# Four recurrent heads in straight-line code, with the next head's projections between the steps of the current one

## What is computed

```
mq, mk = split(silu(centred_short_conv(concat(ml_q, ml_k), conv_w, conv_b)))     # 5 taps in time
h_fwd, h_bwd = mlstm_chunkwise(...), flip(mlstm_chunkwise(flip(...)))              # per head:
    C_new = decay * C + einsum('s,se,sd->ed', w, v_c, k_c)                         #   recurrence over chunks
    S = (q @ k.T) * exp(Dlog - m_t)
    h = (S @ v + inter * (C_prev @ q)) / max(|den|, exp(-m_t))
hm = (h_fwd + h_bwd) * sigmoid(ml_o)
hm = (hm - mean) * rsqrt(var + EPS) * ml_norm_w                                    # per head
ml_out = hm * silu(ml_z)
```

## Time and profile before

| | us |
|---|---|
| three runs | 3822.88, 3825.00, 3828.41 (median 3825.0) |
| the profiled execution | 3826.68, its span 3824.6 |
| `mlstm` in the span: first DMA issue to the next stage's first DMA issue | 193.43 to 1038.64 |
| first matmul of each head | 211.43, 416.98, 625.10, 833.48 |
| TensorE busy over the whole span | 3479.6 (91%) |

### The profile page before, as it was taken

The page is one execution under the profiler, slowest core; times in us unless marked ns, Lnnn a source line. Parts: engine busy times, 40 slices in busy tenths (PEclk is TensorE's granted clock), DMA queues, the critical chain, the costliest instruction groups (busy, mean ns, idle before and its releaser), DMA issues. The chain is left out here.

```text
span 3824.6 us, 43828 instructions
## 1 busy us (share of the span) xinstructions
PE 3479.6 (91%) x16583; PEld 1882.9 (49%) x16583; DVE 1142.0 (30%) x2614; ACT 1013.8 (27%) x2401; POOL 706.5 (18%) x602
## 2 busy tenths in 40 slices
PE   6479797979699999989899999999999999989899
PEld 3238484746545545444445454454545444544444
DVE  3322324142403213154423233242333223211132
ACT  3202112131313324133223342252334233301000
POOL 0010102020100000053331124114211511300143
PEclk9689898989899999999899999999999999999999
DMA  6021001000221010133215615353542445332221
GB/s 226 7 48 28 23 19 29 17 29 23 44 67 32 17 31 18 14 117 102 70 31 34 37 52 88 42 38 85 51 30 43 109 31 40 101 108 92 92 80 67
DMA packets 295199, 211.39 MB, mean 55 GB/s; under 512 B 133401, under 2 KB 261928, under 8 KB 290090
## 3 DMA queue, kind: packets, MB, share of 16 engines
q1 hardware_dynamic: 288726, 198.13, 26.5%
q10 hardware_dynamic: 6272, 10.49, 0.8%
HBM read 166.96 MB, written 41.62 MB: 55 GB/s over the span
## 5 line engine op out<-in xcount | busy, mean ns | idle before, releaser
L1906 PE MATMUL d<-hT,w_tiles 128*128 128x512 f32 x1280 | 584.0, 600 | 9.8 <-DMA qk_w<-in_k_norm_w 9.8
L989 PE MATMUL n<-hT,wo 128*128 128x512 f32 x1024 | 453.4, 601 | 21.5 <-issue 11.6
L1906 PE MATMUL d<-w_room,w_tiles 128*128 128x512 f32 x960 | 433.8, 594 | 0.0
L1906 PEld LDWEIGHTS d<-hT,w_tiles 128*128 128x128 f32 x1280 | 244.5, 192 | 313.2 <-issue 301.5
L563 PE MATMUL m<-hT,w 128*128 128x512 f32 x768 | 341.4, 608 | 34.9 <-PEq L473 18.9
L989 PEld LDWEIGHTS n<-hT,wo 128*128 128x128 f32 x1024 | 194.6, 193 | 259.9 <-issue 248.3
L1906 PEld LDWEIGHTS d<-w_room,w_tiles 128*128 128x128 f32 x960 | 180.6, 190 | 220.6 <-issue 218.8
L563 PEld LDWEIGHTS m<-hT,w 128*128 128x128 f32 x768 | 149.5, 195 | 224.8 <-issue 224.8
L568 PEld LDWEIGHTS m<-w,hT 128*128 128x128 f32 x2048 | 229.3, 192 | 1.9 <-issue 1.9
L568 PE MATMUL m<-w,hT 128*128 128x128 f32 x2048 | 229.3, 275 | 0.0
L2980 PE MATMUL f<-hT,w_tiles 128*128 128x512 f32 x512 | 221.3, 593 | 5.2 <-ACT mid_out L2830 4.0
(11 more groups left out here) (351 smaller groups left out, 4535.9 us busy)
## 6 DMA issues: line engine op xcount, KB each, us to landing
w_tiles<-in_w_in SPq DMA_DIRECT2D x80, 256.0 KB, 2.9
trig<-in_trig SPq DMA_DIRECT2D x16, 1024.0 KB, 5.0
ada<-in_w_ada SPq DMA_DIRECT2D x6, 2048.0 KB, 19.7
mix_f<-alpha SPq DMA_DIRECT2D x64, 192.0 KB, 6.4
w<-in_w_in SPq DMA_DIRECT2D x20, 512.0 KB, 3.6
xg<-in_x ACTq DMA_DIRECT2D x4, 2048.0 KB, 23.4
rb<-r_rows SPq DMA_DIRECT2D x16, 512.0 KB, 5.4
wo<-in_w_in SPq DMA_DIRECT2D x16, 512.0 KB, 3.7
```

What stands on the lines that cost most here:

```text
L989: last = nc.tensor.matmul(bank[b][:], w[:, s, k], hT[:, k, tb * TB:(tb + 1) * TB], start=(k == 0), stop=(k == KC - 1))
L1906: last = nc.tensor.matmul(bank[self.bank_of(n, j, i)][:], w[:, k], x[k], start=(k == 0), stop=(k == h - 1))
```

## The change

- The loop over heads becomes straight-line code inside one block. Semaphores count on over all four heads, and the barrier, the clearing and the POOL copies between heads go.
- K, Q and Z of the next head are projected between the current head's steps: two units after each of the 15 recurrence products and after each of the 16 chunks (62 units), then 26 units up to the end of tile 10, then two after each of the four blocks of output transposes (8 units). V and O stay behind the tail, as a solid piece. The first head's K, Q and Z stay in one piece, and the last head has nothing to project beside it.
- ACT's evictions of those tiles go between its weighings and chunks: K and Q tiles 0 to 6 there, tile 7 and the first Z tile before the Sqrt of the tail, the other three Z tiles behind it.
- DVE's convolution of the next K goes between the normalisation and the multiplication into `mix`; the one of the next Q between the evictions of V.
- The output transposes use banks 2 and 3 instead of 0 and 1. O's weights go into a part of `mix` that is not yet written.
- The constants come as 18 rows in 4 DMAs, and TensorE turns them onto the partitions. Weights of the first head are loaded one by one by SP, K first, and each is waited for only by its user.

```diff
-            def _(act):
-                for s in range(O_):
-                    act.dma_start(w[:, s], w_v[:, :, (col[s] + 1) * HALF - P:(col[s] + 1) * HALF]).then_inc(consts, 16)
-                for n, row in enumerate(rows):
-                    sp.dma_start(small[:, :, n], row.rearrange("(h p) -> p h", p=P), **slow).then_inc(consts, 16)
+                load(0, K_)
+                sp.dma_start(ident[:], t["ident"]).then_inc(consts, 16)
...
+                for n, rows in ((0, b_rows), (5, w_rows), (15, c_rows), (17, t["ml_norm_w"])):
+                    sp.dma_start(small_rows[n:n + rows.shape[0]], rows).then_inc(consts, 16)
+                for s in range(Q_, NW):
+                    load(0, s)
...
-        with nc.Fori(0, ML_HEADS) as back:
...
-            clear(nc, sems, w_in[0])
+                pe.wait_ge(consts, 5 * 16)
+                for h in range(ML_HEADS):
+                    last = nc.tensor.transpose(bank[2][:, 18 * h:18 * h + 18], small_rows[:, h * P:(h + 1) * P], ident[0:18, 0:18])
+                last.then_inc(small_turned, 1)
+                project(0, 0, NA * KC)
+                for x in range(ML_HEADS):
+                    for n in range(NA, NB):
+                        project_turned(x, n)
+                    pe.wait_ge(k_ready, x + 1)
+                    turn(x, 0)
+                    at = 0
+                    for i in range(NS):
+                        if i + 1 < NS:
+                            turn(x, i + 1)
+                        product(x, i)
+                        project(x + 1, at, at + 2)
+                        at += 2
...
+                    for c in range(NT):
+                        if c + 1 < NT:
+                            scores(x, c + 1)
+                        cross(x, c)
+                        within(x, c)
+                        project(x + 1, at, at + 2)
+                        at += 2
+                    project(x + 1, at, 11 * KC)
                     for b in range(NTB):
+                        turn_out(x, b)
+                        project(x + 1, 11 * KC + 2 * b, 11 * KC + 2 * b + 2)
...
+            def _(act):
+                    for i in range(NS):
+                        weigh(x, i)
+                        if i > 3 and i % 4 == 0:
+                            evict(x + 1, i // 4 - 1)
+                    exps(x, 0)
+                    for c in range(NT):
+                        if c + 1 < NT:
+                            exps(x, c + 1)
+                        scale_cross(x, c)
+                        if c % 4 == 2:
+                            evict(x + 1, 3 + c // 4)
+                    evict(x + 1, 7)
+                    evict(x + 1, 8)
+                    act.wait_ge(stat, 2 * NT * (x + 1))
+                    nc.scalar.activation(rs[:, 0], mv[:, :, 1], ACT.Sqrt, bias=epst[:, 0:1]).then_inc(rooted, 1)
+                    for n in range(9, NA):
+                        evict(x + 1, n)
```

More of the change, by code:

```diff
@@ L401, in mlstm @@
     L = P + 1
+    NS = NT - 1
+    LAST = ML_HEADS - 1
+    heads = list(range(ML_HEADS))[::-1]
     with ExitStack() as ctx:
@@ L483, in _, with load @@
-                sp.dma_start(causal[:], t["causal"]).then_inc(consts, 16)
-                sp.wait_ge(consts, 24 * 16)
-            @block.scalar
-            def _(act):
-                for s in range(O_):
-                    act.dma_start(w[:, s], w_v[:, :, (col[s] + 1) * HALF - P:(col[s] + 1) * HALF]).then_inc(consts, 16)
+                def load(x, s):
+                    if x > LAST:
+                        return
+                    if s == O_ and x == LAST:
+                        sp.wait_ge(proj, NB * x + 4)
+                    elif x > 0:
+                        sp.wait_ge(proj, NB * (x - 1) + 4 * s + 4)
+                    c0 = col[s] * HALF + heads[x] * P
+                    sp.dma_start(weights(x, s), w_v[:, :, c0:c0 + P]).then_inc(w_in[s], 16)
@@ new lines, in _ @@
+                for s in range(Q_, NW):
+                    load(0, s)
+                sp.dma_start(causal[:], t["causal"]).then_inc(causal_in, 16)
+                fetch_bias(0)
+                fetch(0, 0)
+                fetch(0, 1)
+                for x in range(ML_HEADS):
+                    if x == 0:
+                        for s in range(V_):
+                            load(1, s)
+                    if x < LAST:
+                        load(x + 1, V_)
+                        load(x + 1, O_)
+                    fetch_bias(x + 1)
+                    if x < LAST:
+                        load(x + 2, K_)
+                    fetch(x, 2)
+                    fetch(x, 3)
+                    fetch(x + 1, 0)
+                    fetch(x + 1, 1)
+                    if x < LAST:
+                        load(x + 2, Q_)
+                        load(x + 2, Z_)
@@ L542, in _ @@
+                pool.wait_ge(causal_in, 16)
+                for x in range(ML_HEADS):
                     for b in range(NTB):
[L543 to L546, removed]
+                        mask(x, b)
@@ L581, in _ @@
                     for i in range(NS):
                         if i + 1 < NS:
[L583 to L600, removed]
-                    need(pe, carried, 2 * NS)
+                            turn(x, i + 1)
@@ L607, in _ @@
-                        nc.tensor.matmul(bank[4 + c % 2][:, 0:2 * L], qT[:, c * P:(c + 1) * P], state[:, c].rearrange("p d l -> p (d l)"), start=True, stop=True).then_inc(crossed, 1)
-                        need(pe, scored, c + 1)
-                        need(pe, summed, max(c - 1, 0))
-                        for dr in range(2):
-                            last = nc.tensor.matmul(bank[6 + c % 2][:, dr * L:(dr + 1) * L], sd[:, c % 2, dr], v1[:, c], start=True, stop=True)
-                        last.then_inc(inside, 1)
@@ L613, in _ @@
-                    for b in range(NTB):
-                        need(pe, normed, 4 * b + 4)
-                        if b < 2:
-                            need(pe, out_dve, 8)
-                        else:
-                            need(pe, h_out, b - 1)
-                        for j in range(4):
-                            last = nc.tensor.transpose(bank[b % 2][:, j * P:(j + 1) * P], og[:, 4 * b + j], ident[:])
-                        last.then_inc(h_turned, 1)
-                @block.scalar
```

431 lines of the change are left out of this document (285 added, 146 removed).

## The result

| | before | changed |
|---|---|---|
| median of four runs, us | 3823.94 (3820.57 to 3828.41) | 3706.24 (3704.18 to 3710.20) |
| ratio, 95% interval | | 0.9693 (0.9676 to 0.9710) |
| span of the profiled execution, us | 3824.6 | 3705.7 |
| `mlstm`: its first DMA issue to the next stage's, us | 193.43 to 1038.64: 845.2 | 192.60 to 922.79: 730.2 |
| the rest of the span, us | 2979.4 | 2975.5 |

The change is worth 117.7 us; 115.0 of the 118.9 us by which the profiled spans differ lie inside `mlstm`. The forecast was 3711 us with a range of 3700 to 3737.

The account below looks back on a forecast made before the run. Each head was taken as 142 us bound by TensorE and 64 us by serial-chain latencies. A gain of 102.5 us between heads, 114.4 with the start, took 3826.68 to 3712.3, hence 3711 us by the median; range 3700 to 3737.

Parts of the forecast that it names:

- What bounds: Each head: 142 us bound by TensorE in the projections, 64 us bound by latencies of a serial chain.
- Rival 1: Recurrence and chunks: units come on top of the waits instead of filling them; 3752 us, chance 0.06.
- The heads: From one head's first transposes to the next one's: 173.6 us, three times, 520.8 in place of 623.35.
- The stall of the tail: TensorE waits at the third block of output transposes for DVE's first multiplication; taken at 1 us, bounds 0 to 1.8.
- the low clock: TensorE's clock low behind the Sigmoid's wait, ahead of the first weighing; 0.7 us a head, bounds 0 to 1.3.
- The start: Before the first head: fewer DMAs bring the first matmul to 199.5 in place of 211.43; gain 11.9 us.
- The last head: It has nothing beside it to project, so its time stays.
- The sum: Gain of 102.5 us over three stretches between heads, 114.4 us with the start.
- Rival 2: Interleaved stretches: TensorE's clock drops; 3732 us at a mean of 0.94, 3761 at 0.87; chance 0.06.
- Rival 3: Tail: a longer ACT to DVE chain delays the third transpose block 4 to 8 us a head; 3723 to 3735; chance 0.09.
- Rival 4: Interleaved stretches mostly at the low clock level, slower than before; 4045 us at c = 0.5; chance 0.01.
- Rival 5: Start: gains nothing, the rows land as late as their 18 forerunners did; 3723 us, chance 0.06.

Follow-up runs that it names:

- experiment 4: Changed kernel with one unit instead of two behind each recurrence product and each chunk, the missing 31 units in the tail: 3710.03 us.
- experiment 3: Changed kernel without units in recurrence and chunks; 88 units in one piece between last chunk and output transposes, 8 between these: 3743.71 us.
- experiment 5: Changed kernel with the Sigmoid of O behind the third weighing of the recurrence instead of ahead of the first: 3697.27 us.
- experiment 1: Changed kernel with the old start: 18 scattered DMAs for constants, first head's weights issued by ACT, TensorE waiting for all: 3721.05 us.
- experiment 2: Changed kernel, still straight-line, without interleaving: all 96 units of the next head in one piece behind the output transposes: 3789.94 us.
- experiment 7: Changed kernel with the first Z tile's Silu behind the Sqrt of the tail instead of ahead of it: 3706.09 us.
- experiment 8: Changed kernel with the Sigmoid behind the third weighing, two pairs of key transposes ahead of the last O tile, and the Sqrt before the first Z Silu: 3693.57 us.
- experiment 10: On experiment 8, 24 units of the last head's own Z tiles move from the head before into its chunks and tail: 3675.90 us.
- experiment 9: On experiment 2, POOL starts the next head's mask additions only behind DVE's normalisation: 3784.44 us.

## Why the prediction was right

**What bounds.** Right. A filled stretch takes TensorE's work and nothing else: 2.39 and 2.82 us where 2.39 and 2.83 were forecast. Rival 1, units on top of waits, is refuted twice, by these and by experiment 4; the 41 us that it would have cost are what experiment 3 pays. One argument against it was wrong as it stood: that each wait is shorter than the two units in front of it. Two units are 1.72 us and TensorE's longest wait 2.2; it was compared with a whole chunk of 2.83. What held is the other argument, that the engines beside have half of the time free, so that one long wait can be paid from the cover of several chunks; experiment 4 shows it with a unit of 0.86 us a chunk.

**The heads.** 520.8 us were forecast for the three distances, 521.6 measured. The stall of the tail was taken at 1 us and is 0.36, and the low clock, taken at 0.7 us, is 0 in the first and 1.7 in the other two. The first error is 1.9 us too much over three heads, the second 1.2 too little; they nearly cancel, and 1.5 us (0.5 a head) are left without a term of their own.

**The start.** Taken at 6.1 us from the first DMA issue, measured 5.3: a DMA of rows is issued in 0.24 to 0.32 us, not in the 0.56 us taken from the scattered ones of `b_in`. The first matmul moved from 211.43 to 197.89, 13.5 us where 11.9 were forecast, 0.8 of it from the stage ahead.

**The last head** was to stay and did: 61.6 us from its first transposes to the next stage's first DMA issue, 62.5 before.

**The sum.** 114.4 us forecast, 115.0 in `mlstm`. The other 3.9 us of the difference between the spans lie in stages that the change does not touch. The medians moved by 117.7 us, so about 3 of the 5 us by which 3706 lies under 3711 are the luck of these stages, and 1 is the median of before, which stood at 3825.0 when the forecast was made and at 3823.9 with a fourth run.

**Rival 2, the clock.** The interleaved stretches stood at 1.00, with pairs of matmuls in changing banks, but for the first 4 us behind the wait for the first weighing in the second and third head. The rule of the Trainium skill that spoke for it ("TensorE: Matmul & The Clock Gate", section "A second HAM failure mode: psum-queue depth-cycling") needs idle moments between the groups, and the units left none. What clock loss there was followed a real wait, and went with it in experiment 5.

**Rival 3, a late tail**, had its mechanism right (ACT's Silu and Sqrt, then DVE's convolution ahead of the multiplications) and its price wrong: the chain ends 0.36 us late a head, not 4 to 8. **Rival 4** falls with rival 2. **Rival 5** is refuted by the start, and experiment 1 shows what it would have cost.

**What the prediction did not see** is that the order of the tail matters in a second way: the late Sqrt keeps DVE's normalisation clear of POOL's mask additions. Here nothing hung on it.

## What to carry to other kernels

Where one engine is busy through one phase and waits on short chains through the next, put pieces of the first phase between the steps of the second; the time is then the sum of that engine's work, which can be had from start-to-start distances to a few tenths of a per cent before the change is built. Ask how much cover each wait needs: half of it did nearly as well here, and what was saved could go to the one part that still had no cover, the last head (17.7 us). Then look for the waits that are left over at the seams: a large Sigmoid ahead of a small step cost 9 to 10 us, through a wait in each filled head and the low clock behind two of them.

## What the runs showed of the hardware

**DVE and POOL.** DVE's 16 `TENSOR_SCALAR` of 128x128 from and to on-chip memory took 4.18 to 4.20 us with POOL idle or held back, 4.93 and 4.94 us in the two heads of experiment 3 where one of POOL's mask additions of 1.26 us fell beside them, and 6.30 to 6.33 us with three of them beside, in all fifteen such heads of experiments 2, 4, 7, 8 and 10. DVE's four `BATCH_NORM_STATS2` took 0.87 us beside such an addition (experiment 2, 390.98) and 0.87 us without. In experiment 2 the single instruction takes 335 ns in the median and 1300 ns at most:

```profile
L884 DVE TENSOR_SCALAR og<-og,mv,rs x16: 332/335/1300, 392.9 to 398.9; 128x128 f32<-128x128 f32 x16
...
L556 POOL TENSOR_TENSOR rb<-rb,causal x4: 1262/1262/1262, 390.9 to 394.6; 128x512 f32<-128x512 f32 x4
```

So it is not slowed evenly: three of the 16 take 0.54, 1.30 and 1.30 us, each ends within 0.1 us of the end of one of POOL's additions, and the other 13 take their usual 0.33. In experiment 9 none exceeds 346 ns. The Trainium skill, "SBUF — State Buffer", section "Who interferes with whom", says that such an instruction can take a port pair that it shares with GpSimd, and that the one that comes second is blocked for the other's whole instruction. The trace agrees, with 1300 ns against 1262: DVE's instruction is the one that is blocked.

**The clock behind a wait.** A wait of 2.8 us on TensorE was followed by half the clock in some heads and not in others of the same execution: not in the first head of the changed kernel, but in the second and third with 1.7 us of loss each. Over the kernel before, the changed one and experiments 1 to 4, 7 and 9, which all have that wait of 2.8 us in four heads each, the low clock followed in 19 of 32; why in these and not in the others is open. A wait of 0.50 us at the same place was followed by it in none of the four heads of experiment 5.

**The stages around.** With code outside `mlstm` unchanged, its first DMA issue stood between 188.4 and 193.8 us over twelve profiled executions, and what came behind the next stage's first DMA issue took between 2781 and 2788 us. A difference of a few us between two spans says nothing of one stage; the distances inside it, within one kernel and between heads with the same clock, agreed to 0.1 us.
